# Table rows handed out differently over the stages of a hybrid decoder layer: 5 and 11 per attention step for 4 and 9, 2.4 and 3.6 per table block for 2.9

## The reference

```python
def one_chunk(args):                     # 128 tokens, 128 experts each
    xb, ib, gb = args
    act = gelu(einsum('cd,ced->ce', xb, u_tab[ib]))      # u rows: dot products
    return einsum('ce,ced->cd', gb * act, v_tab[ib])     # v rows: weighted sum
```

## Time and profile before

| | |
|---|---|
| median of 3 runs | 3673.4 us (3667.66 to 3679.57) |
| profiled execution | 3680.8 us, of which the span of the trace is 3679.0 us |
| granted TensorE clock, mean | 0.92 |
| PE busy | 3180.4 us, 86% of the span |
| DVE busy | 2665.2 us, 72% |
| POOL busy | 1568.2 us, 43% |
| ACT busy | 837.5 us, 23% |
| stages of group B by the trace (us from the span's start) | FoX units 858 to 1257, sliding steps to 1448, merge to 1720, scores to 1880, first pass to 2863, second pass to 3572, rows and norms behind it to 3679 |

### The profile page before, as it was taken

One profiled execution on the slowest core, in us unless ns is written; L12 is line 12 of the kernel. 1 busy time (PEld: TensorE's weight loads), 2 busy tenths in 40 slices (PEclk: granted clock), 3 DMA queues, 4 the chain that ended last, 5 costly groups with the idle time before them and its releaser, 6 DMA issues.

```text
span 3679.0 us, 40327 instructions
## 1 busy us (share of the span) xinstructions
PE 3180.4 (86%) x14161; PEld 1754.2 (48%) x14161; DVE 2665.2 (72%) x5156; ACT 837.5 (23%) x2013; POOL 1568.2 (43%) x1321
## 2 busy tenths in 40 slices
PE   7588879997998886885899899999999999989980
PEld 5467645674666654542444344444544444333430
DVE  5755539977777765877888896977947874545779
ACT  6334212112121122210110282653810000000000
POOL 5100001114555634543434343434425667777663
PEclk9779989998888888997999999999999999999995
DMA  8468633346888857986879899989899999999996
GB/s 280 136 228 338 234 120 121 115 137 238 272 272 292 288 188 267 389 315 222 309 281 361 287 306 360 331 319 349 304 416 354 393 376 363 336 329 366 408 409 258
DMA packets 313258, 1073.17 MB, mean 292 GB/s; under 512 B 36704, under 2 KB 62944, under 8 KB 309216
## 3 DMA queue, kind: packets, MB, share of 16 engines
q0 software_dynamic: 170704, 606.75, 45.6%
q1 hardware_dynamic: 101904, 363.16, 26.8%
q10 hardware_dynamic: 40448, 100.68, 7.6%
HBM read 931.52 MB, written 138.94 MB: 291 GB/s over the span
## 4 chain that ended last, share of the span: by engine, by line
PE 18%; DMA 15%; POOL 10%; DVE 5%; issue 4%; ACT 1%; DVEq 0%; ACTq 0%; POOLq 0%
PE ps L1787 14%; DMA rows<-v,expert_ids 8%; POOL rows L133 4%; POOL hidden_sums L1752 4%; POOL turned_rows L133 2%; DMA rows<-u,expert_ids 2%; DMA turned_rows<-u,expert_ids 2%; DMA h_side_kept<-mixer_state 1%; DVE rows L162 1%; DMA turned_rows<-v,expert_ids 1%; DVE row_sums L168 1%; PE ps L107 1%; PE ps L108 1%; PE ps L109 1%; DMA mixer_state<-u_t 1%
## 5 line engine op out<-in xcount | busy, mean ns | idle before, releaser
L133 POOL DMA_INDIRECT rows<-u,expert_ids x477 | 578.2, 1212 | 835.9 <-DVE hidden_sums L162 708.0
L1787 PE MATMUL ps<-turned_rows,mixer_state 128*128 128x512 f32 x2048 | 899.1, 598 | 6.1 <-DMA mixer_state<-u_t 5.3
L133 POOL DMA_INDIRECT rows<-v,expert_ids x527 | 604.0, 1146 | 659.1 <-DVE row_sums L168 513.8
L168 DVE SCALAR_TENSOR_TENSOR row_sums<-rows,hidden_sums,row_sums 128x1024 f32<-128x1024 f32 x518 | 654.3, 1281 | 238.3 <-DMA rows<-v,expert_ids 233.4
L1824 PE MATMUL ps<-shared_64k 128*128 128x512 f32 x1536 | 677.7, 604 | 35.7 <-DVE shared_64k L1951 35.6
L1787 PEld LDWEIGHTS ps<-turned_rows,mixer_state 128*128 128x128 f32 x2048 | 387.7, 192 | 477.9 <-issue 468.6
L1824 PEld LDWEIGHTS ps<-shared_64k 128*128 128x128 f32 x1536 | 296.2, 194 | 417.1 <-issue 417.1
L162 DVE CUSTOM_DVE_ANT_0 rows<-rows,x_first 128x1024 f32<-128x1024 f32 x256 | 305.4, 1218 | 33.0 <-DMA rows<-u,expert_ids 30.9
L107 PE MATMUL ps<-x_hi_t_b,shared_64k 128*128 128x384 f16 x912 | 308.9, 339 | 18.6 <-DMA shared_64k<-w_pairs_kept 17.7
L162 DVE CUSTOM_DVE_ANT_0 rows<-rows,branches 128x1024 f32<-128x1024 f32 x221 | 268.3, 1217 | 71.5 <-DMA rows<-u,expert_ids 69.2
L108 PE MATMUL ps<-x_lo_t_b,shared_64k 128*128 128x384 f16 x912 | 307.7, 337 | 0.0
(11 more groups left out here) (526 smaller groups left out, 5003.0 us busy)
## 6 DMA issues: line engine op xcount, KB each, us to landing
mixer_state<-u_t ACTq DMA_DIRECT2D x128, 512.0 KB, 6.8
shared_64k<-v SPq DMA_DIRECT2D x128, 512.0 KB, 7.2
rows<-strips SPq DMA_DIRECT2D x32, 768.0 KB, 7.3
h_kept<-branches ACTq DMA_DIRECT2D x32, 768.0 KB, 10.0
shared_64k<-weights_kept SPq DMA_DIRECT2D x32, 768.0 KB, 9.9
shared_64k<-h_kept SPq DMA_DIRECT2D x32, 768.0 KB, 13.6
shared_64k<-s_pairs_kept SPq DMA_DIRECT2D x32, 512.0 KB, 6.0
rows<-w_t SPq DMA_DIRECT2D x30, 512.0 KB, 5.1
```

The costliest lines, as they stand in the source:

```text
L133: nc.gpsimd.indirect_dma_start(row_tile(M, n), None, A["u" if r < NSEL else "v"], bass.IndirectOffsetOnAxis(ap=M["idx"][:, c, e:e + 1], ax ...
L168: nc.vector.scalar_tensor_tensor(acc[:, e % 2, :], src, hid[:, c % 2, e:e + 1], acc[:, e % 2, :], ALU.mult, ALU.add).then_inc(used, 1)
L1787: m = pe.matmul(ps[:, 4 + u % 4, 0:UT], uk[u % 4][:, k, :], x1t[:, k, :], start=k == 0, stop=k == KD - 1)
```

## The change

Each of the 48 FoX units and of the two steps behind them is given five rows for four, each of the seven sliding steps eleven for nine. In the first table pass `dense_row` gives 2.4 rows a block up to block 105 and 3.6 from there to block 128, for 2.9 throughout; the last choice (chunk 4) is spread over blocks 112 to 140 for 112 to 150.

```diff
-ATT_ROWS = spans_of(PROJ_ROWS[-1][1], [0] + [4] * (N_UNIT_B + 2) + [9] * (GB.nc + 1))
+ATT_ROWS = spans_of(PROJ_ROWS[-1][1], [0] + [5] * (N_UNIT_B + 2) + [11] * (GB.nc + 1))
...
-ROWS_U_BLOCK = 2.9
+ROWS_U_BLOCK = 2.4
+ROWS_U_LATE = 3.6
+LATE_BLOCK = 105
 ROWS_V_BLOCK = 2.1
-CHOICE_SPAN = {5: (0, 20), 6: (24, 47), 7: (52, 75), 3: (82, 105), 4: (112, 150)}
+CHOICE_SPAN = {5: (0, 20), 6: (24, 47), 7: (52, 75), 3: (82, 105), 4: (112, 140)}
...
-    return int(R_SCORE + 4 + ROWS_U_BLOCK * min(u, NBLK) + ROWS_V_BLOCK * max(u - NBLK, 0))
+    return int(R_SCORE + 4 + ROWS_U_BLOCK * min(u, LATE_BLOCK) + ROWS_U_LATE * max(min(u, NBLK) - LATE_BLOCK, 0)
+               + ROWS_V_BLOCK * max(u - NBLK, 0))
```

## The result

The changed kernel takes 3699.4 us (median of its runs), the kernel before 3675.3 in the same series: a ratio of 1.0059 with a 95% interval of 1.0042 to 1.0077, so slower by some 22 us. One run in ten of either kernel took far longer (9101.6 us before, 8433.4 after) and is left out of the ratio; without it the medians are 3673.4 and 3698.3. The forecast was 3679, a difference too small to tell from none, with slower at 0.33.

What follows compares the result with a forecast made beforehand. No engine bounds the whole: PE the table passes, DVE the tail, neither fully the attention. 55 + 9 + 4 − 35 + 16 + 2 − 45 = +6 on the median 3673.4 gave 3679 us, range 3630 to 3720.

Steps and rivals of the forecast that it cites:

- FoX (+55): FoX units in the attention: 48 more rows at 1.14 us of DVE's time each, nothing absorbed, +55 us (bounds 0 and 84).
- Rival B: FoX units: the ring of five tiles sets the unit's length, 1.75 us a row, +29, total 3708; chance 0.20.
- Sliding steps (+9): Two steps behind the units +2 us, first five sliding steps nothing, last two +7 (bounds 3 and 25).
- The sign that the prediction named: Attention: the distance from the first unit to the first sliding step grows by 55 us.
- Windows (−35): First pass: with fewer rows and norms moved, DVE is in time and PE's 35.0 us of waits go (−18 to −44).
- Start of the second pass (+16): Ahead of product 0: fourteen more rows at 1.14 us make DVE later, +16 us (bounds 5 and 33).
- C: Ahead of product 0: fourteen rows at the old pace of 2.36 us, weights' transfers sharing DMA; +17, total 3696; chance 0.10.
- Tail (−45): Behind the last product: 32 fewer rows at 1.405 us each, −45 us (bounds −39 and −56).
- Merge (+4): Merge: chunk 1's Gelu moves between ACT's sigmoids, with two table loads about 3.5 us; +4 (bounds 0 and 8).
- choice 4 (+2): Start of the second pass: the shorter span puts ten blocks' worth of pieces nearer the first products, +2 us (0 to 10).
- A: Attention: DVE's idle time takes the rows in, a quarter of the 55 us is left, total 3639; chance 0.32.
- two other ways to slower: Attention: PE's clock falling after longer waits, +14 us; or one slowly issued gather in each unit, 50 us.

## Why the prediction was right or wrong

**FoX (+55): right in size, half right in its reason.** Across the kernels run here FoX took 388 to 398 us with four rows (six traces, mean 393.9) and 443 to 449 with five (five traces, mean 446.3): 52 us, 1.09 a row, beside the 1.14 that the one-row unit had given. But "what a row occupies DVE, with nothing absorbed" was the wrong reading: DVE time alone is half absorbed, and the transfer brings the other half. The group of one row had shed a row's transfer and its use together. Rival B's mechanism was at work inside the forecast's number. Nor did it matter that the added row stands behind DVE's wait at L1047, which the prediction set against its lower bound of 0: with the odd row ahead of that wait, in one unit of four, FoX takes 448.0 us for 449.4.

**Sliding steps (+9): the step that failed.** I set the first five steps at nothing since DVE waits 2.66 us for PE at L1112 and two rows of 1.23 fit in. I counted DVE's time and left out the landing, though I had the rows' pace without cover, 1.75, from the last two steps. Up to the first L1112 the stretch grew by 3.7 us, over the five stretches from L1112 to L1112 by 12.4 and behind them by 11.5, where the forecast had 2, 0 and 7. The five stretches of the changed kernel show why:

```profile
1336.00:1456.00 120.00, 106.29 (x570) 67.67 (x571) 77.87 (x140) 29.51 (x105) 56.85 (x46) 0.87 0.67 230
```

Of DVE's 77.9 us, 44 rows of 1.23 are 54 (the first of the five holds none), so that a step's own instructions take some 5. Eleven rows at 1.75 are 19: 24 together by this estimate, more than the 21.1 of before, and the four steps with rows took 23.6 to 26.1. All 16 rows cost 1.7 each, 27.6, beyond the upper bound of 25. The sign that the prediction named, from the first unit to the first sliding step, came out at 54.9 for 55: what it missed lies behind that point.

**Windows (−35): right**, −39.5, by the mechanism named: five rows fewer (22 for 27 between the exponentials and the first window; the prediction counted 28), and at the first window the norms, which moving them alone shows to be the greater part there. The waits gave 30.3 of it. PE's busy time fell by another 8, from 938.3 to 929.9 us for the same 2825 matmuls, at a granted clock of 1.00 for 0.98; the prediction had that in its bound of −44 alone. The wait of 9.3 that it gave to the other windows was the first one's; theirs reached 6.5.

**Start of the second pass (+16): right in size**, 13.4, and half right in its reason. DVE's waits from the exponentials to product 0, before and after:

```profile
DVE row_sums L168 <- DMA rows<-v,expert_ids: 29.9, 16, 5.2
DVE rows L162 <- DMA rows<-u,expert_ids: 14.9, 13, 3.1
```

```profile
DVE rows L162 <- DMA rows<-u,expert_ids: 35.0, 33, 2.9
```

For 14 rows more and the closer pieces of choice 4 DVE is busy 122.0 us for 99.6, its waits for landings fall from 44.8 to 35.0, and the stretch grows by 13.4, 0.96 a row. So DVE's own time was the price, and a part of it went into its waits for landings; C's price of 2.36 a row is out. That landings still hold DVE up there, as C said, the earlier exponentials show: a lead of 28 us was lost to them, and DVE's idle time is ruled out as the cause. The prediction had 18 us of DVE's work there (with the 2 for choice 4) where 22.4 came, and nothing for these waits where 9.8 came back, so that the nearness of 13.4 to 16 is in part luck.

**Tail (−45): right**, −41.9; the rows left are a little dearer than 1.405 (71.9 / 49 = 1.47). With 117 rows the tail took 164.7, 1.41 each again; what makes the short tail dearer isn't shown.

**Merge (+4) and choice 4 (+2)** came out as +6.6 and +5.0, for the second pass as a whole; neither was tested alone.

**The rivals.** A is out: the rows cost their full price, though DVE's time alone was half taken in. B's time of 3708 was nearer to 3699 than the forecast, though its price of 1.75 a row was wrong for FoX and near only for the sliding steps, where B had not put it. C's price is out; its landings are there. Of the two other ways to slower that the prediction names, gathers that are issued more slowly did not come, and a lower clock did come in FoX (0.81 for 0.86), at a cost that is not separated. The rest between 3679 and 3699 is the sliding steps' 18 us.

## What to carry to other kernels

A unit of side work that comes with a transfer has to find room twice, in the engine's idle time and in the ring that feeds it. Here a stage paced by another engine took nine such units a step without growing and not eleven; the ring's pace times their number, and the step's own instructions, set against the step's length, would have told so ahead (24 us against 21.1). When an engine is late at a hand-over, look first for what it does ahead of it without need (a norm, a wait for a result that could come sooner): here that gave some 24 us, while moving 66 rows elsewhere cost more than it brought. A natural experiment in a trace gives a price without its cause; a dummy instruction without the transfer splits it.

## What the runs showed of the hardware that was not expected

An instruction of 1.21 us on DVE, 48 times over, lengthened a stage in which DVE was busy 75% by 26 of 58 us: the same time that a real row fills is partly free when it brings no DMA. And with the DMA engines full (415 GB/s at a share of 1.03) 28 us of lead for 76 gathers were lost nearly whole: they landed 10.0 us and more after issue there, for 5.8 in the attention of before.
